# Compression projections as plain fp32 products on the four column groups

## The reference, cut to what matters

```python
def _compress(kv, pe, w1, w2):                      # kv 256 x 2 groups x 64, w1 2048 x 256, w2 256 x 64
    c = kv.reshape(B, S // CMP_STRIDE, CMP_STRIDE, G, D)
    blocks = jnp.concatenate([c[:, :-1], c[:, 1:]], axis=2)   # 15 overlapping windows of 32 tokens
    blocks = blocks + pe[None, None, :, None, :]
    n_cmp = blocks.shape[1]
    flat = blocks.transpose(0, 1, 3, 2, 4).reshape(B, n_cmp, G, CMP_LEN * D)
    return jax.nn.gelu(flat @ w1) @ w2

    # in first_block
    h = h + 0.5 * swiglu(rmsnorm(h), ffn1)
    nq, kc, vc, ksl, vsl, kwn, vwn, ng, sq, sk, sv, ga, gb = split(rmsnorm(h) @ w_in)
    k_cmp, v_cmp = rope(_compress(kc, pe_k, wk1, wk2)), _compress(vc, pe_v, wv1, wv2)
    o_a = gated sum of attention over k_cmp (15 keys), k_slc (256 keys) and k_win (256 keys), 8 heads
    o_b = banded attention with sinks, 8 heads (sq, sk, sv)
    merged = sigmoid(ga) * (o_a @ w_branch_a) + sigmoid(gb) * (o_b @ w_branch_b)
    h = h + merged @ w_out
    h = h + 0.5 * swiglu(rmsnorm(h), ffn2)
```

## Time and profile before

| | |
|---|---|
| median of 3 runs | 1330.22 us (1328.27 to 1330.7) |
| profiled execution | 1329.58 us, of which the span shown by the trace is 1327.8 |
| mean granted TensorE clock | 0.983 of 2.4 GHz |
| TensorE busy | 1289.5 us (97%), 8902 matmul records |
| VectorE busy | 821.1 us (62%) |
| ScalarE busy | 628.8 us (47%) |
| `w_lo` on VectorE (L1314) | 198 instructions, 444.6 us |
| `w_hi` on ScalarE (L963) | 198 instructions, 367.6 us |

### The profile page before, as it was taken

One profiled execution on the slowest core, in us unless ns is written; L12 is line 12 of the kernel. 1 busy time (PEld: TensorE's weight loads), 2 busy tenths in 40 slices (PEclk: granted clock), 3 DMA queues, 4 the chain that ended last, 5 costly groups with the idle time before them and its releaser, 6 DMA issues.

```text
span 1327.8 us, 21675 instructions
## 1 busy us (share of the span) xinstructions
PE 1289.5 (97%) x8902; PEld 1177.9 (89%) x8902; DVE 821.1 (62%) x956; ACT 628.8 (47%) x843; POOL 94.4 (7%) x73
## 2 busy tenths in 40 slices
PE   9999999999989999999999999999999999999997
PEld 7999999789888999999988888999998978899996
DVE  4665556666657555555788756555467986655554
ACT  5444446486424533445644354444464345544443
POOL 0000001100000000002422100000005220000000
PEclk9999999999899999999989899999999989999999
DMA  9565557452226455556514245655643323565551
GB/s 281 184 221 190 185 155 185 127 159 96 96 96 206 159 191 189 190 192 171 170 55 145 64 127 191 191 190 190 183 155 118 117 96 93 164 203 184 184 189 44
DMA packets 173684, 209.94 MB, mean 158 GB/s; under 512 B 24248, under 2 KB 149808, under 8 KB 173488
## 3 DMA queue, kind: packets, MB, share of 16 engines
q1 hardware_dynamic: 173168, 208.52, 49.3%
q10 hardware_dynamic: 448, 0.46, 0.2%
HBM read 207.92 MB, written 1.05 MB: 157 GB/s over the span
## 4 chain that ended last, share of the span: by engine, by line
PE 86%; DVE 5%; ACT 4%; issue 2%; DMA 1%; POOL 1%; SPq 0%; DVEq 0%; POOLq 0%; ACTq 0%
PE bank L1807 70%; PE bank L2258 5%; PE bank L2141 2%; PE bank L1884 2%; DVE w_lo L1314 2%; ACT w_hi L963 2%; PE bank L2055 2%; PE bank L2119 1%; POOL scr L889 1%; PE bank L2127 1%; ACT probs L1251 1%; DMA raw<-in_ffn_up_dram 1%; PE bank L2175 1%; PE bank L1864 1%; DMA raw<-in_ffn_gate_dram 1%
## 5 line engine op out<-in xcount | busy, mean ns | idle before, releaser
L1314 DVE TENSOR_TENSOR w_lo<-raw,w_hi 128x2048 fp32r<-128x2048 f32 (+2 forms) x198 | 444.6, 2247 | 296.2 <-ACT w_hi L963 295.6
L963 ACT ACTIVATE w_hi<-raw 128x2048 fp32r<-128x2048 f32 (+2 forms) x198 | 367.6, 1861 | 239.2 <-PE bank L1807 220.3
L1807 PE MATMUL bank<-n_hi,w_hi 128*128 128x256 f32 x1664 | 477.1, 287 | 3.2 <-DVE n_lo L1771 1.9
L1807 PE MATMUL bank<-n_lo,w_hi 128*128 128x256 f32 x1664 | 473.3, 284 | 0.0
L1807 PE MATMUL bank<-n_hi,w_lo 128*128 128x256 f32 x1664 | 473.1, 284 | 0.0
L1807 PEld LDWEIGHTS bank<-n_hi,w_hi 128*128 128x128 f32 x1664 | 320.1, 192 | 9.4 <-issue 5.6
L1807 PEld LDWEIGHTS bank<-n_lo,w_hi 128*128 128x128 f32 x1664 | 320.2, 192 | 2.3 <-issue 0.5
L1807 PEld LDWEIGHTS bank<-n_hi,w_lo 128*128 128x128 f32 x1664 | 320.0, 192 | 0.0
L1807 PE MATMUL bank<-w_hi,hid_hi 128*128 128x512 f32 (+1 forms) x472 | 181.5, 384 | 1.2 <-DVE hid_lo L1387 1.1
L1807 PE MATMUL bank<-w_lo,hid_hi 128*128 128x512 f32 (+1 forms) x472 | 180.8, 383 | 0.0
L1807 PE MATMUL bank<-w_hi,hid_lo 128*128 128x512 f32 (+1 forms) x472 | 180.2, 382 | 0.0
(11 more groups left out here) (257 smaller groups left out, 1544.6 us busy)
## 6 DMA issues: line engine op xcount, KB each, us to landing
raw<-in_w_ff_dram SPq DMA_DIRECT2D x64, 1024.0 KB, 5.2
raw<-in_w_in_dram SPq DMA_DIRECT2D x31, 1024.0 KB, 5.3
raw<-in_ffn_down_dram SPq DMA_DIRECT2D x22, 1024.0 KB, 4.9
raw<-in_ffn_up_dram SPq DMA_DIRECT2D x21, 1024.0 KB, 5.2
raw<-in_ffn_gate_dram SPq DMA_DIRECT2D x20, 1024.0 KB, 5.2
raw<-in_w_out_dram SPq DMA_DIRECT2D x12, 1024.0 KB, 5.0
raw<-in_w_uq_dram SPq DMA_DIRECT2D x8, 576.0 KB, 4.1
raw<-in_w_in_dram SPq DMA_DIRECT2D x12, 256.0 KB, 3.9
```

The source lines that it names most:

```text
L963: nc.scalar.activation(w_hi[:, s % SPLIT, c0:n], raw[:, s % RING, c0:n], ACT.Copy).then_inc(hi_ready, 1)
L1314: V.tensor_tensor(w_lo[:, s % SPLIT, c0:n], raw[:, s % RING, c0:n], w_hi[:, s % SPLIT, c0:n].bitcast(f32), ALU.subtract).then_inc(lo_ready, 1)
L1807: mm = MM(out, stat(k, a), mov(k, b), start=(first and k == 0 and n == 0), stop=(last and k == K - 1 and n == 2), skip_group_check=True)
```

## The change

The steps `("cmp1", v)` become four, `("cmp1", v, half)`, one slab each. They and `("cmpt", "k")` leave attention's list and stand between the projections; `fill` holds the eight gates alone. A step waits for the slab's load and for `xpe`, not for a split: it multiplies the loaded fp32 slab by the fp32 input. Its eight blocks of 128 rows are eight matmuls of 32 (the last 30) stationary columns by 256, whose outputs go to partitions 32j to 32j+31 of one bank (j = 0 to 3, twice), that is to the four column groups of the array. The bank is 2 for keys and 3 for values. The four partial sums lie on 128 partitions; ScalarE copies them, and `cmpt` multiplies them by `fold` (four identities of 32 below each other), which turns and adds them in one product. Gelu comes after that. `xpe_hi` and `xpe_lo` are gone. Since these slabs are never split, `LO` counts splits apart from slabs, and the load that takes such a slab's place waits for `slab_done` of its step. Their steps take no bank of the rotation 4 to 7, so the bank of every later step that draws from it shifts by two, and the rotations of block 1 before attention use banks 0 and 1 alone.

```diff
@@ -128,10 +128,11 @@
 def schedule():
     S = [("gains", 0), ("split", 0), ("root", 0), ("stat", 0), ("gains", 1), ("ffn1", 0), ("split", 1)]
     S += [("proj", 0, "nq0"), ("root", 1), ("proj", 0, "misc"), ("stat", 1), ("proj", 0, "kcvc"), ("proj", 0, "kk"), ("toks", 0),
-          ("rope", 0, "nq0"), ("proj", 0, "vv"), ("rope", 0, "sk"), ("proj", 0, "sq0"), ("rope", 0, "k"),
-          ("xpe", "k"), ("proj", 0, "nq1"), ("rope", 0, "sq0"), ("xpe", "v"), ("proj", 0, "sq1"), ("rope", 0, "nq1"), ("rope", 0, "sq1")]
-    fill = [("cmp1", "k"), ("cmp1", "v")] + [("gate", n) for n in range(8)]
-    after = {("cmp1", "v"): [("cmpt", "k")], ("gate", 0): [("cmp2", "k"), ("cmpt", "v")],
+          ("rope", 0, "nq0"), ("xpe", "k"), ("proj", 0, "vv"), ("rope", 0, "sk"), ("cmp1", "k", 0), ("proj", 0, "sq0"), ("rope", 0, "k"),
+          ("proj", 0, "nq1"), ("rope", 0, "sq0"), ("cmp1", "k", 1), ("xpe", "v"), ("proj", 0, "sq1"), ("rope", 0, "nq1"),
+          ("cmp1", "v", 0), ("rope", 0, "sq1"), ("cmpt", "k"), ("cmp1", "v", 1)]
+    fill = [("gate", n) for n in range(8)]
+    after = {("gate", 0): [("cmp2", "k"), ("cmpt", "v")],
              ("gate", 1): [("cmp2", "v"), ("rope", 0, "kc")], ("gate", 5): [("cs", 0), ("cs", 1)],
              ("gate", 6): [("ct", 0), ("o", 0, "cmp", 0)], ("gate", 7): [("ct", 1), ("o", 0, "cmp", 1)]}
...
-        cmp_h = rgt[0:2 * NCMP, :, :]
+        cmp_h = rgt
+        fold = sb("fold", [P, 32])
         o_tmp = turn_s
...
-        xpe = wflat[:, 1024:1024 + 480]
+        xpe = wflat[:, 1024:2048].rearrange("p (v c) -> p v c", v=2)
...
         def slab(key, loads=1):
             s = len(slabs)
             SL[key] = s
             slabs.append(key)
+            LO.append((LO[-1] if LO else 0) + (key[0] != "cmp1"))
...
         def job(key, b=None, freed_by=None, of_slab=False):
             if b is None and idle[0] and key[0] in ("rope", "rtok", "toks", "idx", "rank"):
-                b = _small[0] % 4
+                b = _small[0] % (4 if hcount[0] > 4 else 2)
                 _small[0] += 1
...
             elif kind == "cmp1":
-                slab(st + (0,))
-                slab(st + (1,))
-                job(st, of_slab=True)
+                slab(st)
+                if st[2] == 0:
+                    job(st[:2], 2 + "kv".index(st[1]), of_slab=True)
+                READY[st[:2]] = (slab_done, len(slabs))
...
-            if s >= RING:
-                sp.wait_ge(lo_ready, s - RING + 1)
+            if s >= RING and slabs[s - RING][0] == "cmp1":
+                sp.wait_ge(slab_done, s - RING + 1)
+            elif s >= RING:
+                sp.wait_ge(lo_ready, LO[s - RING])
...
             def ahead(s, by=2):
 
                 while nxt[0] <= min(s + by, NSLAB - 1):
-                    split(nxt[0], free=nxt[0] >= SPLIT)
+                    if slabs[nxt[0]][0] != "cmp1":
+                        split(nxt[0], free=nxt[0] >= SPLIT)
                     nxt[0] += 1
...
-                elif kind == "xpe":
-                    v = "kv".index(st[1])
-                    act.wait_ge(xpe_ready, v + 1)
-                    nc.scalar.activation(xpe_hi[:, v, :], xpe, ACT.Copy).then_inc(xpeh_ready, 1)
                 elif kind == "cmp1":
                     v = "kv".index(st[1])
-                    ahead(SL[st + (0,)])
-                    ahead(SL[st + (1,)])
-                    pb = await_bank(act, st)
-                    nc.scalar.activation(cmp_h[:, v, :], pb[0:2 * NCMP, 0:T], ACT.Gelu_apprx_tanh).then_inc(freed(st), 1)
+                    ahead(SL[st])
+                    if st[2]:
+                        pb = await_bank(act, st[:2])
+                        nc.scalar.activation(cmp_h[:, v, :], pb[:, 0:T], ACT.Copy).then_inc(freed(st[:2]), 1)
                 elif kind == "cmpt":
 
                     pb = await_bank(act, st)
                     for m in range(2):
                         src = pb[:, m * P:m * P + 2 * NCMP].rearrange("p (g c) -> p g c", g=2)
                         if st[1] == "k":
-                            last = nc.scalar.activation(gkT[:, m, :, 0:NCMP], src, ACT.Copy)
+                            last = nc.scalar.activation(gkT[:, m, :, 0:NCMP], src, ACT.Gelu_apprx_tanh)
                         else:
-                            last = nc.scalar.activation(gvT[:, m, :, :, 0:NCMP], src.unsqueeze(2).to_broadcast([P, 2, 4, NCMP]), ACT.Copy)
+                            last = nc.scalar.activation(gvT[:, m, :, :, 0:NCMP], src.unsqueeze(2).to_broadcast([P, 2, 4, NCMP]),
+                                                        ACT.Gelu_apprx_tanh)
...
             def ahead(s, by=2):
                 while nxt[0] <= min(s + by, NSLAB - 1):
-                    split(nxt[0])
+                    if slabs[nxt[0]][0] != "cmp1":
+                        split(nxt[0])
                     nxt[0] += 1
...
+                V.tensor_reduce(fold[:, :], con("ident").rearrange("p (j c) -> p c j", j=4), AX.X, ALU.add)
...
-                    if v:
-                        dve.wait_ge(xpel_ready, v)
                     pe0 = GROW["cmp_pe_" + st[1]]
-                    out_v = xpe.rearrange("p (a b g c) -> p a b g c", a=2, b=8, g=2)
+                    out_v = xpe[:, v, 0:480].rearrange("p (a b g c) -> p a b g c", a=2, b=8, g=2)
                     for g in range(2):
                         for a in range(2):
                             src = x2[:, v, g, 16 * a:16 * a + 240].rearrange("p (c b e) -> p b c e", b=8, e=2)[:, :, :, 0]
                             last = V.tensor_tensor(out_v[:, a, :, g, :], src, bc(gains[:, pe0 + 8 * a:pe0 + 8 * a + 8], 8, NCMP), ALU.add)
                     last.then_inc(xpe_ready, 1)
-                    dve.wait_ge(xpeh_ready, v + 1)
-                    V.tensor_tensor(xpe_lo[:, v, :], xpe, xpe_hi[:, v, :].bitcast(f32), ALU.subtract).then_inc(xpel_ready, 1)
                 elif kind == "cmp1":
-                    ahead(SL[st + (0,)])
-                    ahead(SL[st + (1,)])
+                    ahead(SL[st])
...
                 elif kind == "cmp1":
                     v = "kv".index(st[1])
-                    pb = take(pe, st)
-                    pe.wait_ge(xpel_ready, v + 1)
-                    for half in range(2):
-                        s = SL[st + (half,)]
-                        weights(s)
-                        for i in range(8):
-                            c = (8 * half + i) * 30
-                            mm = group(pb[0:2 * NCMP, 0:256], 1, lambda k, lo: (xpe_lo if lo else xpe_hi)[:, v, c:c + 30],
-                                       lambda k, lo: w(s, lo)[:, i * 256:i * 256 + 256], first=(half == 0 and i == 0),
-                                       last=(half == 1 and i == 7))
-                        mm.then_inc(slab_done, 1)
+                    _, _, half = st
+                    pb = bank[JOB[st[:2]][0]] if half else take(pe, st[:2])
+                    pe.wait_ge(xpe_ready, v + 1)
+                    s = SL[st]
+                    pe.wait_ge(raw_ready[s % RING], RAWC[s])
+                    for i in range(0, 8, 4):
+                        for j in range(4):
+                            c = (8 * half + i + j) * 30
+                            n = 32 if c < 450 else 30
+                            mm = MM(pb[32 * j:32 * j + n, 0:256], xpe[:, v, c:c + n], raw[:, s % RING, (i + j) * 256:(i + j) * 256 + 256],
+                                    start=(half == 0 and i == 0), stop=(half == 1 and i == 4), skip_group_check=True)
+                    mm.then_inc(slab_done, 1)
                 elif kind == "cmpt":
                     v = "kv".index(st[1])
                     pe.wait_ge(*free_count(("cmp1", st[1])))
                     pb = take(pe, st)
                     for m in range(2):
-                        mm = nc.tensor.transpose(pb[:, m * P:m * P + 2 * NCMP], cmp_h[:, v, m * P:m * P + P], ident[0:2 * NCMP, 0:2 * NCMP])
+                        mm = MM(pb[:, m * P:m * P + 2 * NCMP], cmp_h[:, v, m * P:m * P + P], fold[:, 0:2 * NCMP], start=True, stop=True)
```

15 lines of the change are left out of this document (7 added, 8 removed).

## The result

The changed kernel takes 1334.2 us (median of 20 runs, 1328.7 to 1338.6), the kernel before 1329.95 (20 runs, 1325.5 to 1332.4). The ratio is 1.0033, 95% interval 1.0023 to 1.0044: slower by 4.3 us, a small loss but clear of noise, where 8 us less were forecast. The profiled execution of the changed kernel took 1332.05 us (span 1330.3), 2.1 us under the median, so it is one of the quicker ones.

A forecast was written before the change was run, and what follows sets the result against it. TensorE was taken to bound the kernel (86% of the chain). 20.5 us gone against 13.0 come gave -7.5, with -0.5 far from the change -8.0 in total, so 1322.2 us; range 1318.8 to 1330.2.

The forecast's parts named there:

- the end of attention: After the last weighted values: 4.0 us remain instead of 5.4; less a 0.3 us wait in the last turn, 1.1 gone.
- The steps: Compression before attention: four steps of 1.1 us, 4.4 in all, replace two projection stages of 11.5 us.
- two rivals on the groups: Compression steps: column groups run two at a time (1324.8 us, chance 0.25) or one after another (1330.0 us, chance 0.14).
- The entry: Into attention: the 2.39 us rotation wait goes, but a late load makes TensorE wait 6.3 us before gate 0, until 268.8.
- The second wait and the middle: From gate 0 on: the 2.1 us wait at 292.08 goes, as TensorE's work of a turn covers VectorE's and ScalarE's.
- the last compressed product with its wait (2.2): Near the end of attention: this 2.2 us and the gate's 5.8 move one turn forward.
- The rival "clock": Compression steps before full projections: granted clock falls under them, giving 1336.9 us, or 1332.0 with two falls; chance 0.08.
- Far from the change: Second block's layers, behind attention: shifted banks change waits at first ffn products, together -0.5 us.
- the two places: First ffn products of the second block: layer 0 loses a 1.15 us wait, layer 1 gains one of 0.6.

The follow-up runs named there:

- e4: Changed kernel with the blocks of three of the four compression steps dealt differently to the column groups (one group, two in turn, four and four); 1333.5 us, one run.
- e7: Changed kernel with splits reaching one slab ahead instead of two at the last compression step; 1332.6 us, ratio 1.0023.
- e2: Changed kernel with the compression steps evenly spaced, one behind each of four projections; 1337.8 us, ratio 1.0066.
- e1: Changed kernel with no gate in the first turn of attention, so the eight gates stand in turns 1 to 8; 1325.4 us, ratio 0.9977.
- e13: Changed kernel with two draws of the bank rotation thrown away, so later steps have the banks of the kernel before; 1333.9 us in one run.
- e3: Changed kernel with the last compressed transposition and product (ct 1, o cmp 1) moved from behind gate 7 to behind the last turn; 1331.0 us, ratio 1.0021.
- e8: Changed kernel with the edits of e10 and e7, and one split ahead instead of two at gates 0 to 3 too; 1328.7 us, ratio 0.9997.
- e10: Changed kernel with both ct and both compressed products moved from behind gates 6 and 7 into the last turn; 1331.4 us, ratio 1.0022.
- e11: Changed kernel with VectorE's copies for ct 0 and ct 1 put ahead of the slab splits they had stood behind; 1326.9 us, ratio 0.9986.
- e12: Changed kernel with e1, e11's order, and one split ahead instead of two at the last compression step and gates 0 to 3; 1318.6 us, ratio 0.9928.
- e6: Kernel before with its own split compression products moved ahead of attention and the eight gates alone as fill; 1338.5 us, ratio 1.0074.
- e14: Changed kernel with the plain fp32 compression steps put back in the first two turns of attention; 1323.7 us, ratio 0.9963.

## Why the prediction was wrong

Most steps of it were right, and one sank it: the end of attention.

- **The steps.** 1.00 us against 1.1, four groups side by side, none of the two rivals on the groups. e4 shows what two groups and one group would have been: 1.85 and 3.57 us from start to next start.
- **The entry.** Gate 0 at 269.83 against 268.8, by the chain that was named. The mechanism was shown in part: e7 takes one split out of the chain and 2.5 us out of the wait; e2 shows the freed place of a compression step as a late load elsewhere.
- **The second wait and the middle.** The wait is gone, as forecast. But the wait at `ct 0` grew from 0.96 to 2.19 us.
- **The end of attention, the step that failed.** The prediction let "the last compressed product with its wait (2.2) move one turn forward", at its old price with 0.96 us of wait, and put all behind gate 7 at full clock ("After the last weighted values there remain ... 4.0 instead of 5.4"). It had said that TensorE's work of a turn covers VectorE's and ScalarE's; at `ct` it does not. It knew that the last turn would have no gate, but priced 0.3 us for that, and did not look at what stands ahead of the copy in a turn with scores. 7.5 us were to be left at the branch products, and -1.9 was: 9.4 us missing. By the profile after: 2.1 us more wait at `ct 1` (3.03 against 0.96); the three sets of weighted values and two of transposes between 362.81 and 376.54 took 13.7 us for 7.2 at full clock (3 x 1.81 and 2 x 0.9), 6.5 more; from L2226 to the branch products 5.2 us where e1 takes 4.0, 1.2 more. These make 9.8; by difference, the terms ahead of them together came out 0.4 better than forecast. The rival "clock" looked for the fall under the new steps. It was the right resource in the wrong place, so that its 1332.0 to 1336.9 us lie around the measured time by luck.
- **Far from the change.** -1.15 and +0.55 at the two places, as forecast. But from the branch products to the end of the span the changed kernel took 948.5 us and the kernel before 948.0, 0.5 more where 0.5 less was forecast. With the spread of this stretch (see e13), the total of this term is not shown.
- **What is left.** The profiled execution is thus 2.5 us slower than before: 1.9 at the branch products and 0.5 behind them. The median lies 2.1 above it. In this execution the clock held behind `ct 0`, which was luck: in the five others that have gate 6 in the same turn (e2, e3, e4, e7, e13) it fell there. That such falls make up the rest of the median is likely but not shown.

When the clock falls here is told by all profiles together. Most `ct` waits are followed by 16 weighted values, whose time from start to next start tells the clock (1.73 us at full). In the 13 profiles in which each `ct` wait stands alone (all but e8 and e10) there are 23 such pairs:

| wait at ct | cases | 16 weighted values behind it |
|---|---|---|
| 0.96 us | 8 | 1.73 us in all |
| 2.19 to 3.03 us | 15 | 2.56 to 3.31 us in 13, 1.73 to 1.74 in 2 |

So behind these waits of over 2 us the clock fell nearly always, but not always. Nor is such a wait the only thing that precedes a fall: in e11 it was one of 1.90 us, in e12 one of 1.98 ahead of full work, under the compressed scores none. What a fall costs depends on what comes next. With a gate behind it, the clock comes back at the gate: gate 6 to gate 7 took 16.8 us in e2, e4 and e7 where it is 13.5 without a fall (the changed kernel), 3 us. With nothing but light work up to the branch, e4 gives the price without a fall, 16.4 us from the end of gate 7 to the branch products. e2, e7, e13 and the changed kernel took 22.1 to 23.2, some 6 us more; e6 took 19.8, as the clock came back among the light products. That the fall is a matter of chance may be part of the spread of the changed kernel, 10 us; its two quickest runs had a mean clock of 0.979, its slowest 0.970. This is a correlation of runs that have no trace each, so it is argued, not shown, and the kernel before, whose `ct` waits were 0.96 in its profile, has 7 us between its 20 runs too. What decides between falling and not falling at the same wait stays open.

The medians add up with e6 and e14: placing +9.4 us, steps -5.3 us in the old placing, both together +4.3; added they would be +4.1.

## What to carry to other kernels

A fill step between light products can be worth more than its own work: it hides the waits around it, and behind a fall the clock came back at it. Before taking fills out, write down which turn each remaining fill stands in, and what is queued ahead of every copy that TensorE waits for there; then price the light products behind such a wait at both clock levels, since a lead may be lost in one turn. A short copy that TensorE waits for belongs ahead of a 2.3 us split on VectorE's queue; then look at what stands behind the moved split, since in e11 the wait came back one step later at 1.90 us.

## What the runs showed of the hardware

Plain fp32 matmuls of 128 rows by 32 columns ran side by side on four column groups: the records of the four groups start some 7 ns apart, and a step of 16 records took 1.00 us, against 3.57 on one group (e4). The fourth group, with its output on partitions 96 to 127, ran beside the others. The weight loads of 0.109 us each (16 of them 1.7 us) did not stretch this.

The Trainium skill (TensorE: Matmul & The Clock Gate, The mechanism) has weight loads overlap with matmuls in flight only where the row group differs. By that the 16 loads would have stood between the matmuls; the trace disagrees, for all 16 share their rows. The same section also lets a load for the background weight buffer go ahead of matmuls in flight; no row here tells whether that is what happened. Its section Measured speedup vs the span model has 2.38 times for three column groups; here four gave 3.57 times.
